# Spreading the SSD's cumulative decays over the partitions: from triangle products to row products

## The reference, cut to what matters

```python
def _ssd(z, xbc, dt_raw, conv_w, conv_b, dt_bias, a_log, d_skip, norm_w):
    ...
    dt = jax.nn.softplus(dt_raw.astype(jnp.float32) + dt_bias)
    a = -jnp.exp(a_log.astype(jnp.float32)) * dt
    ...
    a_cs = jnp.cumsum(a.reshape(Bn, NC, C, G, R), axis=2).transpose(0, 1, 3, 4, 2)
    causal = jnp.tril(jnp.ones((C, C), dtype=bool))
    seg = a_cs[..., :, None] - a_cs[..., None, :]
    lmat = jnp.exp(jnp.where(causal, seg, -jnp.inf))
    cb = jnp.einsum('bclgn,bcsgn->bcgls', Cm, Bm)
    y_diag = jnp.einsum('bcgls,bcgrls,bcsgrp->bclgrp', cb, lmat, xdt)
```

## Time and profile before

| | |
|---|---|
| time, median of 3 runs | 2624.58 us (2623.61 to 2629.33) |
| the profiled execution | 2625.14 us, of it 2623.3 us from the first to the last instruction |
| TensorE busy | 2574.8 us (98%) |
| VectorE busy | 2190.1 us (83%) |
| ScalarE busy | 1543.0 us (59%) |
| mean granted TensorE clock | 0.998 |

### The profile page before, as it was taken

How to read it: one execution, slowest core, us unless ns; L and a number is a source line. 1 busy time by engine, 2 the same in 40 slices (tenths; PEclk the granted TensorE clock), 3 DMA queues, 4 the chain that set the end, 5 groups by cost and what they waited for, 6 DMA issues and landing times.

```text
span 2623.3 us, 37661 instructions
## 1 busy us (share of the span) xinstructions
PE 2574.8 (98%) x15545; PEld 2294.5 (87%) x15545; DVE 2190.1 (83%) x2489; ACT 1543.0 (59%) x1628; POOL 47.9 (2%) x84
## 2 busy tenths in 40 slices
PE   7999999999999999999999999999999999999998
PEld 6889988888888888888888899999999999998998
DVE  6988877799989899999989889985577799863877
ACT  3534345577777777777777755545554566354554
POOL 1010000000000000000000000000000000000000
PEclk9999999999999999999999999999999999999999
DMA  9679955399999999999999954444555534554553
GB/s 328 229 246 368 352 207 178 124 370 372 356 374 362 357 361 371 355 356 364 356 364 359 335 187 146 151 167 139 192 195 180 184 126 137 162 179 157 177 183 114
DMA packets 376784, 670.44 MB, mean 256 GB/s; under 512 B 27161, under 2 KB 199967, under 8 KB 371743
## 3 DMA queue, kind: packets, MB, share of 16 engines
q1 hardware_dynamic: 358624, 662.02, 71.5%
q10 hardware_dynamic: 17983, 5.94, 0.9%
HBM read 663.72 MB, written 4.19 MB: 255 GB/s over the span
## 4 chain that ended last, share of the span: by engine, by line
PE 85%; DVE 7%; ACT 2%; DMA 2%; issue 2%; POOL 0%; ACTq 0%; SPq 0%; POOLq 0%; DVEq 0%
PE PS L464 25%; PE PS L466 24%; PE PS L465 24%; DVE LO L459 3%; PE PS L572 2%; PE PS L2846 2%; PE PS L1758 1%; ACT HI L438 1%; DMA RAW<-in_w_ada_dram 1%; DMA AR<-in_w_ada_dram 1%; PE PS L782 1%; DMA RAW<-in_w_in_dram 1%; PE PS L2734 1%; PE PS L2725 1%; PE PS L2910 1%
## 5 line engine op out<-in xcount | busy, mean ns | idle before, releaser
L459 DVE TENSOR_TENSOR LO<-RAW,HI 128x2048 fp32r<-128x2048 f32 (+1 forms) x407 | 922.4, 2273 | 149.6 <-ACT HI L438 148.0
L438 ACT ACTIVATE HI<-RAW 128x2048 fp32r<-128x2048 f32 x410 | 780.5, 1904 | 331.2 <-PE PS L466 289.7
L464 PE MATMUL PS<-X1H,HI 128*128 128x256 f32 (+1 forms) x2128 | 607.8, 286 | 5.6 <-DVE X1L L656 4.7
L465 PE MATMUL PS<-X1L,HI 128*128 128x256 f32 (+1 forms) x2128 | 603.2, 283 | 0.0
L466 PE MATMUL PS<-X1H,LO 128*128 128x256 f32 (+1 forms) x2128 | 603.1, 283 | 0.0
L464 PE MATMUL PS<-HI,X1H 128*128 128x512 f32 x1056 | 419.1, 397 | 4.3 <-DVE LO L459 2.9
L464 PEld LDWEIGHTS PS<-X1H,HI 128*128 128x128 f32 (+1 forms) x2128 | 407.8, 192 | 10.0 <-issue 5.7
L466 PE MATMUL PS<-HI,X1L 128*128 128x512 f32 x1056 | 412.0, 390 | 0.0
L465 PE MATMUL PS<-LO,X1H 128*128 128x512 f32 x1056 | 411.5, 390 | 0.0
L465 PEld LDWEIGHTS PS<-X1L,HI 128*128 128x128 f32 (+1 forms) x2128 | 408.1, 192 | 1.6
L466 PEld LDWEIGHTS PS<-X1H,LO 128*128 128x128 f32 (+1 forms) x2128 | 407.8, 192 | 0.4
(11 more groups left out here) (424 smaller groups left out, 2810.3 us busy)
## 6 DMA issues: line engine op xcount, KB each, us to landing
RAW<-in_w_in_dram SPq DMA_DIRECT2D x66, 1024.0 KB, 5.5
RAW<-in_expert_w_gate_dram SPq DMA_DIRECT2D x66, 1024.0 KB, 7.0
RAW<-in_expert_w_up_dram SPq DMA_DIRECT2D x65, 1024.0 KB, 7.2
RAW<-in_expert_w_down_dram SPq DMA_DIRECT2D x61, 1024.0 KB, 7.1
RAW<-in_ffn_w_up_dram SPq DMA_DIRECT2D x55, 1024.0 KB, 5.7
AR<-in_expert_w_down_dram SPq DMA_DIRECT2D x51, 1024.0 KB, 7.2
AR<-in_expert_w_up_dram SPq DMA_DIRECT2D x47, 1024.0 KB, 7.1
AR<-in_expert_w_gate_dram SPq DMA_DIRECT2D x46, 1024.0 KB, 7.2
```

The costliest lines, as they stand in the source:

```text
L438: a.activation(HI[:, n % NH, 0:size(i)], raw_at(i), ACT.Copy).then_inc(*hi.up(i))
L459: v.tensor_tensor(LO[:, m % NH, 0:n], raw_at(i), HI[:, m % NH, 0:n].bitcast(F32), ALU.subtract).then_inc(*lo.up(i))
L464: t.matmul(o, lh, rh, start=first, stop=False)
L465: t.matmul(o, lh, rl, start=False, stop=False)
```

## The change

The sums in `CS` are transposed once for each layer into PSUM bank 3 (16 partitions, 128 columns), and ScalarE copies them into a new buffer `CSR` (step "csr"). For each head two products replace the three: a selector, one column of the identity's first 16 rows spread over 128 weight columns, times `CSR`. They work on 16 rows of the array. `logits(1)` waits for "csr" where it waited for "cs", since bank 3 is then free; TensorE waits for "cs" ahead of the new transpose, which stands between the "v" transposes and `turn_x(2)`; ScalarE's new copy stands between the copy of the values and `ev_xs(2)`. `SM` grows from 640 to 656 columns, and holds `CSR` besides the small buffers.

```diff
-    SM = sb("SM", [128, 640])
+    SM = sb("SM", [128, 656])
...
+    CSR = sm(128)
...
             if h == 1:
-                t.wait_ge(*dve_mix("cs", l))
+                t.wait_ge(*act_mix("csr", l))
...
         def decay(h):
             b = 4 + h % 2
-            col = lambda k: view(AA[:, 8 * k + h:8 * k + h + 1], [0, 128])
+            row = lambda k: view(ident[0:16, 8 * k + h:8 * k + h + 1], [0, 128])
+            t.wait_ge(*act_mix("csr", l))
             t.wait_ge(*(dve_mix("e8", l, h - 2) if h > 1 else act_mix("xs", l, 2 + h)))
-            t.matmul(PS[:, b, 0:128], col(0), tri, start=True, stop=True)
-            t.matmul(PS[:, b, 128:256], col(0), ones, start=True, stop=False)
-            t.matmul(PS[:, b, 128:256], col(1), tri, start=False, stop=True).then_inc(*pe_mix.up("e8", l, h))
+            t.matmul(PS[:, b, 0:128], row(0), CSR[0:16, :], start=True, stop=True)
+            t.matmul(PS[:, b, 128:256], row(1), CSR[0:16, :], start=True, stop=True).then_inc(*pe_mix.up("e8", l, h))
...
             *pe_mix.up("v", l))
+        t.wait_ge(*dve_mix("cs", l))
+        turn(t, [(PS[0:16, 3, 128:256], CS)]).then_inc(*pe_mix.up("csr", l))
         turn_x(2)
         turn_x(3)
...
             *act_mix.up("v", l))
+        a.wait_ge(*pe_mix("csr", l))
+        a.activation(CSR[0:16, :], PS[0:16, 3, 128:256], ACT.Copy).then_inc(*act_mix.up("csr", l))
         ev_xs(2)
         ev_xs(3)
```

More of the change, by code:

```diff
@@ L281, in sm @@
         sm_at[0] += n
-        assert sm_at[0] <= 640
+        assert sm_at[0] <= 656
         a = SM[:, o:o + n]
```

## The result

The changed kernel takes 2634.78 us (median of 7 runs, 2628.72 to 2636.18) against 2624.58 (7 runs, 2623.17 to 2629.33): ratio 1.0031, 95% interval 1.0021 to 1.0041. It is slower by some 8 us by the ratio (10.2 between the two medians), where +0.9 was forecast, and lies above the range of 2621 to 2629.

The account below looks back on a forecast made before the run. TensorE was taken to bound the second layer and the experts, VectorE the first layer. First layer +1.5 and second layer -0.56 sum to +0.94 us: 2625.5 on the median of 2624.58, range 2621 to 2629.

Parts of the forecast that it names:

- Everything else costs nothing: Outside the counted terms: ScalarE's copy, the wait for "cs" and the DMAs were said to add no time.
- something unseen: Catch-all outcome for effects the prediction did not name, chance 0.04.
- The wait in the first layer: `logits(1)` waits for ScalarE's late copy; first decay 1.77 us late, layer 1.5 us longer after 0.27 saved.
- That the clock falls: Rival: TensorE's first-layer standstill lowers the granted clock, costing 1.65 us more, 2627.2 in all; chance 0.17.
- the new standstill is nearer to the earlier trace: First layer: some 2 us standstill judged nearer 196.00 to 200.00 (no clock loss) than 60.00 to 63.60 (clock fell).
- VectorE sets the pace of the first layer: First layer: VectorE works without a gap from 82 us, but for 1.28 us; TensorE's savings ahead of 106.45 gain nothing.
- The second layer: TensorE holds the chain there: wait 0.33, products saved 1.79, setting changes 0.90, together -0.56 us.
- five changes: Five more switches of TensorE's row setting in a layer, 0.18 us each, 0.90 us; 0.36 at the low end.
- 16 rows to 64: Switch from 16-row products to 64-row `logits` and `ret_scores`; no row showed it, taken at the full 0.18 us.
- The saving passes in both layers: Rival: TensorE's clean sum holds everywhere without waits or setting changes, -3.36 us, 2621.2; chance 0.07.
- The wait is hidden: Rival: first-layer weight timing shrinks the delay, first layer -0.27 at best, sum -0.8, 2623.8; chance 0.12.

Follow-up runs that it names:

- run 2: Changed kernel with 44 never executed TensorE instructions in the skipped body, so the jump lands as in the kernel before: 2628.89 us, ratio 1.0013.
- run 3: Kernel before with 212 never executed TensorE instructions in the skipped body, so the jump lands as in the changed kernel: 2629.37 us, ratio 1.0017.
- first profile: Profiled execution of the changed kernel in its first measurement, the shortest of its seven: 2628.72 us.
- run 1: The changed kernel once more without an edit, for a second trace: 2634.04 us, ratio 1.0030.
- run 5: Changed kernel with the sums' transpose and ScalarE's copy put earlier, and 44 never executed instructions keeping the old landing: 2627.38 us, ratio 1.0004.
- run 6: Changed kernel with early transpose and copy, old landing, `SM` at 640 columns and `CSR` in a free stretch of the arena: 2625.63 us, ratio 0.9999.
- run 7: Kernel before with `SM` at 656 columns and nothing else: 2625.51 us, ratio 1.0000.
- run 9: Changed kernel, old landing, with four idle TensorE products between `logits(0)` and `logits(1)` of the first layer: 2628.29 us, ratio 1.0006.
- run 4: Changed kernel with 12 never executed instructions in the skipped body, so the jump lands 2 instructions ahead of a transfer's end: 2638.03 us, ratio 1.0043.
- run 8: Kernel before with the new transpose, copy and wait of `logits(1)`, but the three old products of each decay: 2631.37 us, ratio 1.0021.
- run 10: Changed kernel with early copy, old landing, `SM` at 640 columns and three idle products at the start of layer 1: 2625.34 us, ratio 0.9993.

## Why the prediction was wrong

**The sum had two places; the time changed in four.** The runs take the change's 0.3% apart one step at a time: 1.0030 as it is, 1.0013 with the old landing, 1.0004 without the wait as well, 0.9999 with the buffers in their places too. The intervals overlap from step to step, but each step has its place in the traces.

1. *"Everything else costs nothing".* This step failed most. It went through waits, copies and DMAs; it didn't ask what 44 instructions fewer do to the place of the program, though the product records that go were counted. Runs 2 and 3 show the price in both directions: some 4.5 us by the ratios; in the traces +4.7, +4.6 and +3.4 at the jump (first profile, runs 1 and 3), of which 2.5 to 2.7 are the stop and the rest is the clock behind it. It was only inside "something unseen", at 0.04.

2. *The size of `SM`.* The diff shows 640 to 656 and the prediction gave it no term. Runs 5, 6 and 7 show +0.9 us over the experts, from `PPT` lying 64 bytes further on.

3. *The wait in the first layer.* The wait's own part was forecast at 1.77 us for the first decay and measured 2.16 (run 9); in that profile the weights came half a microsecond later than in the trace used. That the clock falls had been a rival with 0.17 and a price of 1.65, and its sign, a lower clock near 84 us, came. The price was about right (1.6 to 2.7 in runs 1, 2 and 4), the chance was not: the clock fell in all of them and in run 8. The step that failed is the judgement that the new standstill is nearer to the earlier trace rows than to the earlier trace rows. The trace of the kernel before had a third place, which the prediction left out: TensorE waits 1.78 us, less than the new wait was expected to last, and the clock falls behind it (timeline, then windows).

```profile
173.48 0.45 PE L464 MATMUL PS<-X1H,HI 128*128 128x256 f32 x1 [1.78 <-DVE X1L L656]
```

```profile
172.00:176.00 4.00, 2.52 (x12) 2.55 (x13) 3.84 (x8) 4.00 (x8) 0.00 (x0) 0.70 1.10 365
```

Nor is the earlier trace rows a safe place: the clock fell there in runs 5, 9 and 10, at some 1.5 us each, behind waits of 2.2 to 2.6 us; it stayed in the other ten profiles, some with waits as long. That VectorE sets the pace of the first layer held where the wait is gone: in run 5 it takes up the first decay without waiting for TensorE. With the wait it stands for TensorE there (0.96 us in the first profile, 2.48 in run 1).

4. *The second layer.* Forecast -0.56, measured -0.52 to -0.56 in the changed kernel's profiles. The parts hold too: 0.22 us a product; the wait alone +0.24 (run 8, forecast 0.33), hence the products and changes -0.77 (forecast -0.89), so some 0.20 for each of five changes, 0.18 forecast. That 16 rows to 64 costs as much as the others, which no row of before showed, is seen at 88.48 to 88.79 (0.31, as from 128 rows to 64 in the kernel before, 88.13 to 88.44). The Trainium skill, "TensorEngine Tiling (Array Packing)", section Tiling Modes, Key Properties, has a change of the mode drain TensorE; the trace agrees as far as a price goes, for 16 to 64 rows too.

5. *The rivals.* "The saving passes in both layers" (-3.36) fell: even run 6, free of all three losses, has -0.73 in the second layer and about -0.2 at the first decay. "The wait is hidden" was the execution profiled first, in which the weights came 2.39 us after the residual's start (3.57 before, 4.18 in run 1); it stayed the exception.

## What to carry to other kernels

When a change adds or removes instructions, count them for each engine and look at where its taken jumps land; if the trace shows an idle stretch that ends with "issue" in a place that the diff doesn't touch, add code that isn't executed until the landing is as it was, and compare again before blaming the change. When an engine has nothing to do in a new wait, give the lower clock behind it a large chance in the price, and put the step that it waits for ahead of anything that depends on a transfer. Give a new small buffer a place that leaves the others where they are.

## What the runs showed of the hardware

- TensorE's program is fetched in parts of 16,384 bytes. Behind a taken jump it stopped for 2.46 to 2.69 us with 14 instructions left to a part's end, for some 4 us with 2 left (5.60 less the 1.4 to 1.7 that are a wait anyway), and not at all with 226.
- Behind the new wait of the first layer, 1.52 to 2.54 us in runs 1, 2, 4 and 8, the granted clock fell to half each time, and the first decay came 0.6 to 2.7 us later than in run 9; with a wait of 0.77 us (first profile) or with idle products in it (run 9) the clock stayed at 1.00.
- The length of a wait doesn't settle it alone: behind the waits of 1.5 and 1.8 us at the start of layer 1 the clock fell in runs 2 to 6 and stayed in the kernel before, the first profile and runs 1, 7, 8 and 9.
- Products whose weights lie in a buffer moved by 64 bytes took 398 and 392 ns in place of 389, and slowed some that follow.
